# One part of a two-block network: low parts of two projections and the skip product move from VectorE to GpSimd, the decay rows' DMAs from GpSimd to SyncE

## The chip, the cores and the metric

One core of one Trainium2 chip. The metric is the device time of one launch in microseconds, the median over the runs. The engines: TensorE (PE) multiplies matrices, VectorE (DVE), ScalarE (ACT) and GpSimd (POOL) work on tiles, SyncE (SP) only issues DMAs here, GpSimd issues a few as well.

## The reference

Two network blocks for 256 tokens of width 1024, all in float32. The first has retention and attention and a PEER layer (product-key experts); the second has a SwiGLU, a mixer, another SwiGLU and a gated per-layer embedding. The change lies in the mixer of the second block:

```python
proj = n @ w_in[i]
u, v, z, xbc, dt_raw = jnp.split(proj, IN_SPLITS_2, axis=-1)
ya = chunked_spatial_gating(jax.nn.gelu(u, approximate=False), jax.nn.gelu(v, approximate=False), ...)
ya = rmsnorm(ya, gm_out_norm[i])
yb = mamba2_mixer(z, xbc, dt_raw, conv_w[i], conv_b[i], dt_bias[i], a_log[i], d_skip[i], ssm_norm[i])
h = h + jnp.concatenate([ya, yb], axis=-1) @ w_out[i]
...
xbc = jax.nn.silu(causal_depthwise_conv(xbc, conv_w, conv_b))
dt = jax.nn.softplus(dt_raw.astype(f32) + dt_bias.astype(f32))
y = ssd_chunked(xs, dt, a, bm, cm) + xs * d_skip.astype(f32)[:, None]
```

`ssd_chunked` takes exponentials of differences of the cumulated decays (16 heads, two chunks of 128 tokens), masks them and multiplies with C B^T, and that with x dt. The last line's second term is the skip product.

## The kernel before

The kernel streams all weights once from DRAM, in 257 chunks of 1 MB (`wall`, 128 x 2048 floats), through a ring of three buffers (`raw`). Each chunk is two halves, called units and numbered 0 to 513 through the whole program. A float32 matmul is done in three passes at float32r: the weights are split into a high part `w_hi` (ScalarE's copy of `raw`, rounded) and a low part `w_lo = raw - w_hi`, and the activations likewise (tiles `HX`, `HC`). Both parts have a ring of `NH` = 4 halves. The road of one unit: SyncE loads the chunk (`sync_program`; it waits until the low parts of the chunk three back are made), ScalarE makes the high part (`ahead` in `scalar_program`; it waits until TensorE has used the unit four back), and VectorE, or GpSimd if the unit is in the set `LO_POOL`, makes the low part (`ahead` in `vector_program` and `gpsimd_program`). TensorE begins a unit with the matmuls of the high part (semaphore `s_hi`) and waits for the low part (`LOW[u]`, counted by `s_lov` for VectorE, `s_lop` for GpSimd) before the last third. `ahead(u)` makes parts up to three units beyond u (`REACH`, `AHEAD` = 3), one after the other in the engine's own order.

Before the change `LO_POOL` holds 27 units, all between the first block's query projection and the first PEER units, where VectorE seeks the top 16.

The mixer has three stretches. The xBC projection (`U_XBC`, units 386 to 397) gives six bank loads of two blocks of 128 features, c = 0 to 5; for each VectorE evacuates the bank with the norm's factor (`tt(xbT..)`, signal `s_xb`), ScalarE makes the first of four taps of the convolution, VectorE the other three (`convolved(m)`, twelve m, three `stt` of 128x256 each), and ScalarE the Silu (`activated(m)`). TensorE needs the evacuation of pair c before pair c + 2. At c = 1 the softplus of dt is made, in small steps that go back and forth between VectorE and ScalarE. The second projection (`U_IN2`, units 398 to 421) has six groups of four units: v, v, u, u (Gelu) and z, z (Silu). Beside them the rest of the mixer is done, in steps named in the table `SIDE`: one row for each unit from 398 on, which all engines go through in the same order, each doing its own share. The names that matter: `silu` and `conv` are the last convolved blocks; `xt` and `xs` turn x to token rows; `cb` and `cbs` are C B^T; `xdt` is x dt; `dec` makes the differences of decays for four heads from `R`, rows of the cumulated decays broadcast to all partitions; `exp` and `mt` make the masked matrix from them, `heads` multiplies it with xdt; `xd` is the skip product (in place in `xs`), `y` adds it to the heads; `vneg` to `vc` are the layer norm of v, `gm` and `gmu` the spatial gate, `ub..` and `yb..` the blocks of the output projection (`U_OUT2`, units 422 to 437).

`R` comes by DRAM: GpSimd waits for ScalarE's copy of the turned decays (`s_act`), writes 16 KB to `acs_keep` and reads two broadcasts of 1 MB back:

```python
p.wait_ge(s_act, 1)
e.dma_start(acs_keep.rearrange("(h t) -> h t", h=16), acT[0:16, :, :].rearrange("p a b -> p (a b)")).then_inc(s_keep, 16)
p.wait_ge(s_keep, 48)
for b in range(2):
    e.dma_start(R[b], acs_keep[b * 2048:(b + 1) * 2048].partition_broadcast(128)).then_inc(s_R, 16)
```

The instructions are written by helpers, so that the profile has one line for many: L923 is every matmul, L1524 every ScalarE operation, L1992 every `tensor_tensor` of VectorE, L1997 and L1999 `tensor_scalar`, L2004 `scalar_tensor_tensor`, L2769 GpSimd's low part. Nearly all working tiles lie in one arena and are called `ar` in the profile. Each engine waits for its own last result before the next instruction (`settle`), but where a call says `free`.

Of the kernel before, what the change touches and what calls it, by code (L numbers as in the profile page):

```python
# [122 lines left out]
def ffn_at(base, c):  # L123
# [8 lines left out]
           | set(range(U_PEER + 20, U_PEER + 25)))  # L132
# [196 lines left out]
def group_done(g):  # L329
# [17 lines left out]
    [("act", 0), ("silu", 8), ("conv", 10)],  # L347
# [12 lines left out]
    [("heads", 4), ("xd", 0)],  # L360
    [("xd", 1), ("y", 0)],
# [43 lines left out]
def program(nc, wall, keys_d, cols_d, rows_d, bigrows_d, crow_d, wmod_d, dist_d, x_d, ctx_d, pT_d, gws_d, out_d, n_chunks):  # L405
    assert n_chunks * 2 == U_END
    with ExitStack() as es:
# [36 lines left out]
        class Arena:  # L444
# [3 lines left out]
            def get(self, *shape, dt=None):  # L448
# [10 lines left out]
                if len(shape) == 3:  # L459
# [1054 lines left out]
        def scalar_program(e):  # L1514
# [387 lines left out]
            def beside(name, n):  # L1902
# [13 lines left out]
                elif name == "vsq":  # L1916
                    a.wait_ge(s_vc, 1)
                    for i in range(2):
                        act(m_y[:, i, :], m_v[:, i, :], ACT.Square, bias=lnst[:, i:i + 1], acc=lnst[:, 2 + i:3 + i],
                            sig=s_vsq)  # L1920
                elif name == "vroot":
                    a.wait_ge(s_vv, 1)
                    act(lnst[:, 2:4], lnst[:, 2:4], ACT.Sqrt, sig=s_vs)
                elif name == "usq":
                    a.wait_ge(s_um, 4)
                    for i in range(2):
                        act(big[:, i * 1024:(i + 1) * 1024], m_u[:, i, :], ACT.Square, acc=lnst[:, 4 + i:5 + i],
                            sig=s_usq)
                elif name == "uroot":
                    a.wait_ge(s_uv, 1)  # L1930
                    act(lnst[:, 4:6], lnst[:, 4:6], ACT.Sqrt, sig=s_us)
                elif name == "ubh":
                    high(TB_U + n)
                elif name == "ysq":
                    for g_ in range(2):
                        a.wait_ge(s_yz, 2 * g_ + 2)
                        for i in range(2):
                            act(big[:, i * 1024 + g_ * 512:i * 1024 + (g_ + 1) * 512], m_y[:, i, g_ * 512:(g_ + 1) * 512],
                                ACT.Square, acc=lnst[:, 6 + 2 * i + g_:7 + 2 * i + g_], sig=s_ysq)
                elif name == "yroot":  # L1940
                    a.wait_ge(s_yv, 1)
                    act(lnst[:, 6:10], lnst[:, 6:10], ACT.Sqrt, sig=s_ys)
                elif name == "ybh":
                    high(TB_Y + n)
# [40 lines left out]
        def vector_program(e):  # L1985
# [622 lines left out]
            def beside(name, n):  # L2608
# [9 lines left out]
                elif name in ("xdt", "xd"):  # L2618
                    xv = xs[:, n, :].rearrange("p (h d) -> p h d", d=64)
                    if name == "xdt":  # L2620
                        v.wait_ge(s_xs, 4)
                        tt(xdt[:, n, :].rearrange("p (h d) -> p h d", d=64), xv, bc(dt[:, n, :], 2, 64), MUL, sig=s_xdt)
                    else:
                        tt(xv, xv, bc(row("dskip"), 2, 64), MUL)
# [20 lines left out]
                elif name == "y":  # L2645
                    s_ = slice(n * 512, (n + 1) * 512)
                    v.wait_ge(s_yh, 2 * n + 2)
                    for i in range(2):
# [6 lines left out]
                elif name == "vvar":  # L2655
                    v.wait_ge(s_vsq, 2)
                    ts(lnst[:, 2:4], lnst[:, 2:4], 1.0 / 1024, EPS, MUL, ADD, sig=s_vv)
                elif name == "vrcp":
                    v.wait_ge(s_vs, 1)
# [13 lines left out]
                elif name == "uvar":  # L2673
                    v.wait_ge(s_usq, 2)
                    ts(lnst[:, 4:6], lnst[:, 4:6], 1.0 / 1024, EPS, MUL, ADD, sig=s_uv)
                elif name == "uscale":
                    v.wait_ge(s_us, 1)
# [10 lines left out]
                elif name == "yvar":  # L2688
                    v.wait_ge(s_ysq, 4)
                    ts(lnst[:, 6:10], lnst[:, 6:10], 1.0 / 512, EPS, MUL, ADD, sig=s_yv)  # L2690
                elif name == "yscale":
                    v.wait_ge(s_ys, 1)
# [62 lines left out]
        def gpsimd_program(e):  # L2755
# [37 lines left out]
            p.did(e.memset(xbT[:, :, 0:4], 0.0), s_set)  # L2793
            p.wait_ge(s_big, 32)
# [127 lines left out]
```

## Time and profile before

| | us |
|---|---|
| median of 3 runs | 1695.77 |
| lowest, highest | 1695.45, 1696.73 |
| profiled execution, its span from first to last instruction | 1695.0 |
| TensorE matmuls busy | 1631.9 (96%) |
| VectorE busy | 1270.3 (75%) |
| ScalarE busy | 967.3 (57%) |
| GpSimd busy | 72.6 (4%) |

The profiled execution has no separate end-to-end time; its span lies 0.8 us under the median of the runs. Busy shares overlap: an engine can be busy all the time and set nothing. What sets the time is read from the waits of TensorE, stage by stage.

### The profile page before, as it was taken

Reading aid. Unit: us, or ns where it says so; the run is one execution under the profiler, and the core shown is the slowest. Engines: PE = TensorE matmul, PEld = TensorE weight load, DVE = VectorE, ACT = ScalarE, POOL = GpSimd, SP = SyncE. Lnnn points to the kernel's source line nnn. Section 1 sums busy time; section 2 is a strip of 40 time slices with the busy share of each in tenths; the row PEclk is TensorE's granted clock in tenths of the full one; section 3 lists DMA queues with packets and bytes.
Section 4 is the critical chain, followed back from the end, with each engine's and each line's share of the span. In section 5 each row is a group of like instructions: output and inputs, shape, how many; then the busy total and the mean of one; then the engine's idle time right before and its main releaser. Section 6 shows DMA issues by size and latency. Waiting matters only on the chain.

```text
span 1695.0 us, 26902 instructions
## 1 busy us (share of the span) xinstructions
PE 1631.9 (96%) x10312; PEld 1392.9 (82%) x10312; DVE 1270.3 (75%) x2044; ACT 967.3 (57%) x1342; POOL 72.6 (4%) x46
## 2 busy tenths in 40 slices
PE   7999889998999999999999999999998989999997
PEld 2777679998999888888888888788888778788886
DVE  3668766999888999987777666776667887676666
ACT  5546655554555454555555555655556867655556
POOL 0000007520000000000000000000000000000000
PEclk9999889999999999999999999999999999999999
DMA  8644235446555455566655555455543533555552
GB/s 336 253 173 160 90 120 192 162 166 208 192 185 191 174 192 213 193 255 219 219 208 210 214 198 197 152 199 192 197 179 139 223 124 128 202 199 179 198 195 75
DMA packets 53266, 317.86 MB, mean 188 GB/s; under 512 B 5937, under 2 KB 6097, under 8 KB 19218
## 3 DMA queue, kind: packets, MB, share of 16 engines
q1 hardware_dynamic: 51954, 310.08, 51.3%
q0 software_dynamic: 1184, 6.05, 0.9%
q8 instruction: 82, 1.34, 0.3%
q14 instruction: 46, 0.38, 0.1%
HBM read 306.65 MB, written 9.47 MB: 186 GB/s over the span
## 4 chain that ended last, share of the span: by engine, by line
PE 79%; DVE 14%; ACT 4%; DMA 2%; issue 1%; SPq 0%; DVEq 0%; ACTq 0%; POOL 0%
PE pb L923 78%; DVE w_lo L1992 4%; DVE ar L1992 4%; ACT ar L1524 2%; DVE ar L2004 2%; DVE ar L2373 1%; ACT w_hi L1524 1%; DVE ar L2370 1%; DMA raw<-in_wall 1%; DMA ar<-acs_keep 1%; DVE ar L2377 1%; ACT L1524 0%; DVE ar L2148 0%; DVE ar L2008 0%; DVE sm L2226 0%
## 5 line engine op out<-in xcount | busy, mean ns | idle before, releaser
L1992 DVE TENSOR_TENSOR w_lo<-raw,w_hi 128x1024 fp32r<-128x1024 f32 x471 | 577.0, 1225 | 174.5 <-ACT w_hi L1524 143.2
L1524 ACT ACTIVATE w_hi<-raw 128x1024 fp32r<-128x1024 f32 x498 | 528.7, 1062 | 153.2 <-PE pb L923 112.8
L923 PE MATMUL pb<-HX,w_hi 128*128 128x256 f32 (+1 forms) x2752 | 509.1, 332 | 7.6 <-DVE HX L1992 3.4
L923 PEld LDWEIGHTS pb<-HX,w_hi 128*128 128x128 f32 x2752 | 413.8, 192 | 50.9 <-issue 3.9
L923 PE MATMUL pb<-w_hi,HC 128*128 128x512 f32 (+1 forms) x1648 | 444.5, 391 | 2.9 <-DVE HC L2004 1.8
L923 PEld LDWEIGHTS pb<-w_hi,HC 128*128 128x128 f32 x1648 | 302.7, 189 | 64.0 <-issue 3.9
L1524 ACT ACTIVATE ar<-pb 128x256 f32<-128x256 f32 (+2 forms) x320 | 152.6, 477 | 328.5 <-PE pb L923 226.0
L1992 DVE TENSOR_TENSOR ar<-ar 128x512 bf16<-128x512 bf16 (+9 forms) x506 | 268.6, 566 | 43.8 <-ACT ar L1524 19.9
L923 PE MATMUL pb<-HX,w_lo 128*128 128x256 f32 x1952 | 279.8, 284 | 2.5 <-DVE w_lo L1992 2.2
L923 PEld LDWEIGHTS pb<-HX,w_lo 128*128 128x128 f32 x1952 | 264.4, 192 | 14.5 <-DVE w_lo L1992 3.3
L923 PE MATMUL pb<-w_lo,HC 128*128 128x512 f32 (+1 forms) x824 | 253.2, 389 | 0.0
L923 PEld LDWEIGHTS pb<-w_lo,HC 128*128 128x128 f32 x824 | 154.8, 189 | 32.5
L923 PE MATMUL pb<-w_hi,HX 128*128 128x512 f32 x512 | 141.5, 398 | 2.8 <-ACT w_hi L1524 2.0
L923 PE MATMUL pb<-ar 128*128 128x64 bf16 (+3 forms) x1960 | 122.6, 222 | 10.9 <-issue 3.6
L923 PEld LDWEIGHTS pb<-ar 128*128 128x128 bf16 (+2 forms) x1960 | 103.4, 119 | 32.5 <-issue 21.7
L923 PEld LDWEIGHTS pb<-w_hi,HX 128*128 128x128 f32 x512 | 93.2, 188 | 23.1 <-ACT w_hi L1524 3.1
L1524 ACT ACTIVATE HC<-ar 128x512 fp32r<-128x512 f32 (+1 forms) x89 | 55.4, 623 | 83.3 <-PE pb L923 46.9
L1992 DVE TENSOR_TENSOR ar<-pb,ar 128x512 f32<-128x512 f32 (+1 forms) x86 | 58.4, 679 | 52.6 <-ACT ar L1524 44.6
L1524 ACT ACTIVATE ar<-ar 128x512 f32<-128x512 f32 (+7 forms) x108 | 66.1, 612 | 55.6 <-DVE ar L1992 31.5
L1992 DVE TENSOR_TENSOR HC<-ar,HC 128x512 fp32r<-128x512 f32 (+1 forms) x89 | 60.5, 680 | 32.8 <-ACT HC L1524 28.1
L923 PE MATMUL pb<-w_lo,HX 128*128 128x512 f32 x256 | 79.7, 392 | 0.6 <-DVE w_lo L1992 0.3
L2769 POOL TENSOR_TENSOR w_lo<-raw,w_hi 128x1024 fp32r<-128x1024 f32 x27 | 64.8, 2401 | 104.1 <-ACT w_hi L1524 91.5
(148 smaller groups left out, 674.3 us busy)
## 6 DMA issues: line engine op xcount, KB each, us to landing
raw<-in_wall SPq DMA_DIRECT2D x257, 1024.0 KB, 4.8
ar<-in_wmod SPq DMA_DIRECT2D x24, 512.0 KB, 4.3
act_keep<-ar SPq DMA_DIRECT2D x28, 256.0 KB, 5.6
ar<-act_keep SPq DMA_DIRECT2D x28, 256.0 KB, 5.0
x<-in_wmod SPq DMA_DIRECT2D x8, 512.0 KB, 5.6
ar<-in_bigrows POOLq DMA_DIRECT2D x2, 1024.0 KB, 5.1
ar<-acs_keep POOLq DMA_DIRECT2D x2, 1024.0 KB, 9.0
x<-in_x SPq DMA_DIRECT2D x1, 1024.0 KB, 12.1
```

Of the source, the lines that this page charges most:

```text
L923: return e.matmul(o, l, r, start=start, stop=stop, skip_group_check=True)
L1524: a.did(e.activation(out, in_, func, scale=scale, **kw), sig)
L1992: v.did(e.tensor_tensor(out, a_, b_, op), sig)
L2004: v.did(e.scalar_tensor_tensor(out, a_, s_, b_, op0, op1), sig)
L2370: v.did(e.max(vals[:, c_], src))
L2373: v.did(e.max_index(idx[:, c_], vals[:, c_], src))
L2377: v.did(e.match_replace(src, vals[:, c_], src, NEG))
L2769: p.did(e.tensor_tensor(w_lo[:, made % NH, :], raw_half(w), w_hi[:, made % NH, :].bitcast(F32), SUB), s_lop)
```

## The change

Units 388 to 421 join `LO_POOL`: all but the first two low parts of the xBC projection and all of the second projection's are GpSimd's. The skip product `xd` leaves `SIDE` and VectorE and becomes `skipped(i)` on GpSimd, ahead of the low parts of units 409 and 412; `y` waits for both (`s_xd`). GpSimd's affine select (the causal mask of the gate's weights) now stands behind four low parts. The DMAs of the decay rows are issued by SyncE, after the chunks of units 406 and 408. In `SIDE` the step `conv 11` moves up by one unit and `silu 11` from the fourth row to the third, so that it stands before the first Gelu. Semaphores of the variances are merged (one counter for several steps, with the counts to match), which is left out below.

```diff
 LO_POOL = (set(range(U_QUERY + 4, U_PEER + 5)) | set(range(U_PEER + 7, U_PEER + 12))
-           | set(range(U_PEER + 20, U_PEER + 25)))
+           | set(range(U_PEER + 20, U_PEER + 25)) | set(range(U_XBC + 2, U_IN2 + 24)))
...
 SIDE = [
-    [("act", 0), ("silu", 8), ("conv", 10)],
-    [("xt", 0), ("xt", 1), ("silu", 9), ("conv", 11)],
-    [("xt", 2), ("xt", 3), ("xs", 0), ("silu", 10)],
-    [("xt", 4), ("xt", 5), ("xs", 1), ("silu", 11)],
+    [("act", 0), ("silu", 8), ("conv", 10), ("conv", 11)],
+    [("xt", 0), ("xt", 1), ("silu", 9)],
+    [("xt", 2), ("xt", 3), ("xs", 0), ("silu", 10), ("silu", 11)],
+    [("xt", 4), ("xt", 5), ("xs", 1)],
     [("xt", 6), ("xt", 7), ("xs", 2), ("dec", 0)],
...
-    [("heads", 4), ("xd", 0)],
-    [("xd", 1), ("y", 0)],
+    [("heads", 4)],
+    [("y", 0)],
...
                 e.dma_start(raw[:, n % NRAW, :], wall[n]).then_inc(s_raw[n % NRAW], 16)
+                if n == U_IN2 // 2 + 4:
+                    e.wait_ge(s_act, 1)
+                    e.dma_start(acs_keep.rearrange("(h t) -> h t", h=16),
+                                acT[0:16, :, :].rearrange("p a b -> p (a b)")).then_inc(s_ckeep, 16)
+                if n == U_IN2 // 2 + 5:
+                    e.wait_ge(s_ckeep, 32)
+                    for b in range(2):
+                        e.dma_start(R[b], acs_keep[b * 2048:(b + 1) * 2048].partition_broadcast(128)).then_inc(s_R, 16)
...
                     v.wait_ge(s_yh, 2 * n + 2)
+                    v.wait_ge(s_xd, 2)
                     for i in range(2):
                         tt(m_y[:, i, s_], PB[4 + i][:, :], xs[:, i, s_], ADD, sig=s_y)
...
             p.did(e.memset(xbT[:, :, 0:4], 0.0), s_set)
+            ahead(U_XBC + 2)
             p.wait_ge(s_big, 32)
             p.settle()
             p.did(e.affine_select(out=gw, in_=gw, pattern=[[0, 8], [1, 128]], compare_op=ALU.is_ge, fill=0.0, base=0,
                                   channel_multiplier=-1), s_set)
-            p.wait_ge(s_act, 1)
-            e.dma_start(acs_keep.rearrange("(h t) -> h t", h=16), acT[0:16, :, :].rearrange("p a b -> p (a b)")).then_inc(s_keep, 16)
-            p.wait_ge(s_keep, 48)
-            for b in range(2):
-                e.dma_start(R[b], acs_keep[b * 2048:(b + 1) * 2048].partition_broadcast(128)).then_inc(s_R, 16)
+
+            def skipped(i):
+
+                xv = xs[:, i, :].rearrange("p (h d) -> p h d", d=64)
+                p.settle()
+                p.did(e.tensor_tensor(xv, xv, bc(row("dskip"), 2, 64), MUL), s_xd)
+
+            ahead(U_IN2 + 7)
+            p.wait_ge(s_xdt, 2)
+            skipped(0)
+            ahead(U_IN2 + 10)
+            skipped(1)
+            ahead(U_IN2 + 20)
             p.wait_ge(s_res, result(N_F2, 1, 1))
```

VectorE before, from the last full set of six convolution steps (`ar<-ar,cols`) through the two half sets of `conv 10` and `conv 11` to the decays of `dec 0` (128x4 to 128x1024) and the first of `cbs`:

```order
L2004 SCALAR_TENSOR_TENSOR ar<-ar,cols 128x256 x6
L1992 TENSOR_TENSOR w_lo<-raw,w_hi 128x1024
L2004 SCALAR_TENSOR_TENSOR ar<-ar,cols 128x256 x3
L1992 TENSOR_TENSOR w_lo<-raw,w_hi 128x1024
L2004 SCALAR_TENSOR_TENSOR ar<-ar,cols 128x256 x3
L1992 TENSOR_TENSOR w_lo<-raw,w_hi 128x1024 x3
L1992 TENSOR_TENSOR ar<-ar 128x4
L1992 TENSOR_TENSOR ar<-ar 128x4x2x128
L1992 TENSOR_TENSOR ar<-ar 128x512
L1997 TENSOR_SCALAR ar<-ar 128x1024
L1992 TENSOR_TENSOR w_lo<-raw,w_hi 128x1024 x2
L1992 TENSOR_TENSOR ar<-pb,cols 128x2x128 x2
```

The same place in the change:

```order
L2011 SCALAR_TENSOR_TENSOR ar<-ar,cols 128x256 x12
L1999 TENSOR_TENSOR ar<-ar 128x4
L1999 TENSOR_TENSOR ar<-ar 128x4x2x128
L1999 TENSOR_TENSOR ar<-ar 128x512
L2004 TENSOR_SCALAR ar<-ar 128x1024
L1999 TENSOR_TENSOR ar<-pb,cols 128x2x128 x2
```

Every `w_lo` row is gone, and convolution steps and decays stand next to each other. GpSimd in the change, from the DMAs of the mixer's constants on (before, the rows with `w_lo` and with `ar<-ar,rows` were not there, and three DMAs with `acs_keep` stood behind the affine select):

```order
L2796 DMA ar<-in_bigrows 128x2048
L2797 DMA ar<-in_gws 128x1024
L2798 MEMSET ar 128x12x4
L2774 TENSOR_TENSOR w_lo<-raw,w_hi 128x1024 x4
L2802 AFFINE_SELECT ar<-ar 128x1024
L2774 TENSOR_TENSOR w_lo<-raw,w_hi 128x1024 x17
L2809 TENSOR_TENSOR ar<-ar,rows 128x1024
L2774 TENSOR_TENSOR w_lo<-raw,w_hi 128x1024 x3
L2809 TENSOR_TENSOR ar<-ar,rows 128x1024
L2774 TENSOR_TENSOR w_lo<-raw,w_hi 128x1024 x10
L2818 DMA ar<-in_bigrows 128x2048
```

The two skip products stand between low parts, so that whatever they wait for holds up the low parts behind them.

## Rows read from the trace of the kernel before

**Rows 1.** The page: span and busy time of each engine.

```profile
span 1695.0 us, 26902 instructions
...
PE 1631.9 (96%) x10312; PEld 1392.9 (82%) x10312; DVE 1270.3 (75%) x2044; ACT 967.3 (57%) x1342; POOL 72.6 (4%) x46
```

**Rows 2.** Busy time by stretch: stretch, length, engines, granted clock (1.00 is full), DMA.

```profile
1306.70:1310.30 3.60, 3.59 (x19) 3.59 (x20) 2.91 (x6) 3.33 (x6) 0.00 (x0) 0.61 0.00 0
...
1343.00:1358.20 15.20, 15.16 (x68) 12.39 (x68) 13.13 (x14) 12.12 (x14) 0.00 (x0) 1.00 0.50 192
...
1386.00:1390.00 4.00, 4.00 (x19) 3.92 (x20) 3.86 (x5) 0.00 (x0) 0.00 (x0) 0.57 0.33 135
```

**Rows 3.** Timeline of TensorE: start, duration, what [idle before it, releaser].

```profile
1306.71 3.17 PE L923 MATMUL pb<-HX,w_hi 128*128 128x256 f32 x16 [2.37 <-DVE ar L1992]
...
1343.04 1.57 PE L923 MATMUL pb<-ar 128*128 128x256 f32 x8 [1.83 <-ACT ar L1524]
...
1347.19 1.07 PE L923 MATMUL pb<-w_hi,HX 128*128 128x512 f32 x4
...
1349.91 1.07 PE L923 MATMUL pb<-w_hi,HX 128*128 128x512 f32 x4
...
1386.00 3.65 PE L923 MATMUL pb<-ar 128*128 128x128 f32 x16 [3.35 <-DVE ar L1992]
...
1414.49 0.62 PE L923 MATMUL pb<-w_lo,HX 128*128 128x512 f32 x2
```

**Rows 4.** Timeline of VectorE in the convolutions.

```profile
1305.97 0.69 DVE L1992 TENSOR_TENSOR ar<-pb,fsc 128x512 f32<-128x512 f32 x1
...
1313.92 0.69 DVE L1992 TENSOR_TENSOR ar<-pb,fsc 128x512 f32<-128x512 f32 x1
1314.72 3.15 DVE L2004 SCALAR_TENSOR_TENSOR ar<-ar,cols 128x256 f32<-128x256 f32 x6
1317.98 2.55 DVE L1992 TENSOR_TENSOR w_lo<-raw,w_hi 128x1024 fp32r<-128x1024 f32 x2
```

**Rows 5.** Groups of VectorE by shape, 1283 to 1409: busy us, mean ns | idle before.

```profile
L1992 DVE TENSOR_TENSOR w_lo<-raw,w_hi 128x1024 fp32r<-128x1024 f32 x33 | 40.4, 1225 | 17.9 <-ACT w_hi L1524 15.3
L2004 DVE SCALAR_TENSOR_TENSOR ar<-ar,cols 128x256 f32<-128x256 f32 x36 | 17.4, 484 | 2.5 <-DVE w_lo L1992 0.5
L1992 DVE TENSOR_TENSOR ar<-ar 128x1024 f32<-128x1024 f32 x6 | 7.3, 1225 | 0.3
L1992 DVE TENSOR_TENSOR ar<-ar 128x1536 f32<-128x1536 f32 x3 | 5.3, 1758 | 0.3
L2004 DVE SCALAR_TENSOR_TENSOR ar<-ar 128x1024 f32<-128x1024 f32 x4 | 5.1, 1285 | 0.2
...
L1997 DVE TENSOR_SCALAR ar<-ar 128x1024 f32<-128x1024 f32 x4 | 2.8, 694 | 0.1
L1992 DVE TENSOR_TENSOR ar<-ar 128x512 f32<-128x512 f32 x4 | 2.8, 691 | 0.1
```

**Rows 6.** Timeline, VectorE and GpSimd in the first block's top-16 stretch.

```profile
319.96 2.71 DVE L2370 MAX8 ar<-ar 128x8 f32<-128x256 f32 x8
320.01 12.60 POOL L2769 TENSOR_TENSOR w_lo<-raw,w_hi 128x1024 fp32r<-128x1024 f32 x5 [10.14 <-DVE w_lo L1992]
```

**Rows 7.** Timeline around GpSimd's affine select.

```profile
1280.68 1.11 POOL L2796 TENSOR_SCALAR_AFFINE_SELECT ar<-ar 128x1024 f32<-128x1024 f32 x1 [5.30 <-DMA ar<-in_gws]
...
1281.14 0.73 DVE L1997 TENSOR_SCALAR fsc<-cols,sm 128x128 f32<-128x128 f32 x1
...
1282.18 0.29 DVE L1997 TENSOR_SCALAR fsc<-cols,sm 128x128 f32<-128x128 f32 x1
```

**Rows 8.** Timeline of ScalarE between the first Gelu and the last Silu.

```profile
1341.28 1.28 ACT L1524 ACT_TABLE_LOAD   x1
```

**Rows 9.** The decay rows: GpSimd's issue (timeline), and a link of the chain of waits.

```profile
1332.11 0.50 POOL L2799 DMA_DIRECT2D acs_keep<-ar  x1 [50.31 <-ACT ar L1524]
...
1334.60 10.83 DMA ar<-acs_keep
```

More of the change, by code:

```diff
@@ L1919, in beside @@
                         act(m_y[:, i, :], m_v[:, i, :], ACT.Square, bias=lnst[:, i:i + 1], acc=lnst[:, 2 + i:3 + i],
-                            sig=s_vsq)
+                            sig=s_sq)
                 elif name == "vroot":
-                    a.wait_ge(s_vv, 1)
-                    act(lnst[:, 2:4], lnst[:, 2:4], ACT.Sqrt, sig=s_vs)
+                    a.wait_ge(s_var, 1)
+                    act(lnst[:, 2:4], lnst[:, 2:4], ACT.Sqrt, sig=s_root)
                 elif name == "usq":
@@ L1927, in beside @@
                         act(big[:, i * 1024:(i + 1) * 1024], m_u[:, i, :], ACT.Square, acc=lnst[:, 4 + i:5 + i],
-                            sig=s_usq)
+                            sig=s_sq)
                 elif name == "uroot":
-                    a.wait_ge(s_uv, 1)
-                    act(lnst[:, 4:6], lnst[:, 4:6], ACT.Sqrt, sig=s_us)
+                    a.wait_ge(s_var, 2)
+                    act(lnst[:, 4:6], lnst[:, 4:6], ACT.Sqrt, sig=s_root)
                 elif name == "ubh":
@@ L1938, in beside @@
                             act(big[:, i * 1024 + g_ * 512:i * 1024 + (g_ + 1) * 512], m_y[:, i, g_ * 512:(g_ + 1) * 512],
-                                ACT.Square, acc=lnst[:, 6 + 2 * i + g_:7 + 2 * i + g_], sig=s_ysq)
+                                ACT.Square, acc=lnst[:, 6 + 2 * i + g_:7 + 2 * i + g_], sig=s_sq)
                 elif name == "yroot":
-                    a.wait_ge(s_yv, 1)
-                    act(lnst[:, 6:10], lnst[:, 6:10], ACT.Sqrt, sig=s_ys)
+                    a.wait_ge(s_var, 3)
+                    act(lnst[:, 6:10], lnst[:, 6:10], ACT.Sqrt, sig=s_root)
                 elif name == "ybh":
@@ L2617, in beside @@
                     cp(cbs[:, :, 256:384], PB[4][:, :].rearrange("p (a b) -> p a b", a=2)[:, :, 128:256], sig=s_cbs)
[L2618 to L2624, printed above, removed]
+                elif name == "xdt":
+                    v.wait_ge(s_xs, 4)
+                    tt(xdt[:, n, :].rearrange("p (h d) -> p h d", d=64), xs[:, n, :].rearrange("p (h d) -> p h d", d=64),
+                       bc(dt[:, n, :], 2, 64), MUL, sig=s_xdt)
                 elif name == "dec":
@@ L2655, in beside @@
                 elif name == "vvar":
-                    v.wait_ge(s_vsq, 2)
-                    ts(lnst[:, 2:4], lnst[:, 2:4], 1.0 / 1024, EPS, MUL, ADD, sig=s_vv)
+                    v.wait_ge(s_sq, 2)
+                    ts(lnst[:, 2:4], lnst[:, 2:4], 1.0 / 1024, EPS, MUL, ADD, sig=s_var)
                 elif name == "vrcp":
-                    v.wait_ge(s_vs, 1)
+                    v.wait_ge(s_root, 1)
                     rcp(lnst[:, 2:4], lnst[:, 2:4])
@@ L2673, in beside @@
                 elif name == "uvar":
-                    v.wait_ge(s_usq, 2)
-                    ts(lnst[:, 4:6], lnst[:, 4:6], 1.0 / 1024, EPS, MUL, ADD, sig=s_uv)
+                    v.wait_ge(s_sq, 4)
+                    ts(lnst[:, 4:6], lnst[:, 4:6], 1.0 / 1024, EPS, MUL, ADD, sig=s_var)
                 elif name == "uscale":
-                    v.wait_ge(s_us, 1)
+                    v.wait_ge(s_root, 2)
                     rcp(lnst[:, 4:6], lnst[:, 4:6])
@@ L2688, in beside @@
                 elif name == "yvar":
-                    v.wait_ge(s_ysq, 4)
-                    ts(lnst[:, 6:10], lnst[:, 6:10], 1.0 / 512, EPS, MUL, ADD, sig=s_yv)
+                    v.wait_ge(s_sq, 8)
+                    ts(lnst[:, 6:10], lnst[:, 6:10], 1.0 / 512, EPS, MUL, ADD, sig=s_var)
                 elif name == "yscale":
-                    v.wait_ge(s_ys, 1)
+                    v.wait_ge(s_root, 3)
                     rcp(lnst[:, 6:10], lnst[:, 6:10])
```

8 lines of the change are left out of this document (3 added, 5 removed).

## The prediction

> **What bounds the kernel now.** I read the page first: the span is 1695.0 us, and TensorE is busy for 96% of it, VectorE for 75%, GpSimd for 4% [rows 1]. So on the whole TensorE sets the time, and a change elsewhere is worth only what TensorE waits for. The next view is the table by stage, and in it the mixer, from the first unit of the xBC projection (1276 us) to the last unit of the second projection (1416 us). I number the halves of weight chunks as the program does: xBC is units 386 to 397, the second projection 398 to 421. The change hands 388 to 421 to GpSimd. TensorE has three holes here worth naming, and the timeline of TensorE tells who ended them. It stands for 2.37 us before 1306.71, and VectorE's evacuation of a bank (ar from pb) ends it; for 1.83 us before 1343.04, ended by ScalarE (the Silu of the last convolved block); for 3.35 us before 1386.00, ended by VectorE (the y sums) [rows 3]. Behind the first and the third the granted clock is 0.61 over 3.6 us and 0.57 over 4 us, where it is 1.00 in the undisturbed stretch from 1343 to 1358 [rows 2]: the clock has fallen to its lower level for a part of those stretches. That costs about 0.39 x 3.6 = 1.4 and 0.43 x 4 = 1.7 us more. With some 1.5 us of holes under 0.7 us, about 12 us can be had in this stage and no more. A unit of the second projection takes 2.72 us where nothing is late (1347.19 to 1349.91) [rows 3].
>
> VectorE is what is late. In the convolutions its rhythm for two units is 0.69 (bank) + 3.15 (six convolution steps) + 2.55 (two low parts) and the gaps, from 1313.92 over 1314.72 and 1317.98 to 1320.53, some 6.7 us with the gap to the next bank [rows 4].
>
> **The change, part by part.**
>
> Low parts off VectorE: 34 of 1.225 us, 33 of them (40.4 us) between 1283 and 1409 [rows 5], and two skip products, by the row of the same shape 1.22 each. VectorE is given back 44 us.
>
> Low parts on GpSimd: the two-input subtraction of 128x1024 takes 2.40 there, and five in a row take 12.60, so (12.60 - 2.40) / 4 = 2.55 us from start to start [rows 6]. 34 of them are 86.7 us, two skip products of the same shape 5.1. GpSimd must make one in each 2.72 us of TensorE; alone on its road it can, just. ScalarE's high parts come up to four units ahead, so the 1.2 us more per low part are covered by that lead (8 us).
>
> The road. GpSimd and VectorE both read and write SBUF, and one place of this trace shows them together on instructions of the kind that matter: GpSimd's affine select (1.11 us from 1280.68) ends at 1281.79, and VectorE's TENSOR_SCALAR of 128x128 that began at 1281.14 takes 0.73 us, ending at 1281.87. The same instruction one microsecond later takes 0.29 [rows 7]. It stood still until GpSimd was done. Against that, GpSimd's 27 low parts of before keep their 2.40 us, but beside them VectorE ran only MAX8 and its kin, with one input [rows 6]. No row shows a VectorE instruction with two SBUF inputs beside a low part on GpSimd, and such ones are nearly all that VectorE keeps here. Bounds for them: free of each other (the 27 low parts' 2.40), or one after the other (the TENSOR_SCALAR). I take one after the other. The row is nearer: both instructions want SBUF operands at full rate, while the MAX8 rows want one stream.
>
> The Trainium skill (SBUF — State Buffer, Who interferes with whom) says the same in general: a VectorE instruction with two SBUF inputs, or in a mode that uses both its ports, and a GpSimd instruction that reads SBUF exclude one another for a whole instruction. By that rule the sum is the slower one below; if the rule were wrong for two inputs, it would be the first rival's. This trace agrees for the 0.73 us row; for two inputs no run here shows it yet.
>
> The sum for the excluded road. From 1283 on GpSimd needs it for 33 x 2.55 + 5.1 = 89.3 us. VectorE needs it for 17.4 (36 convolution steps) + 7.3 + 5.3 + 5.1 + 2.8 + 2.8 (decays, products, layer norm) [rows 5], and about 4.7 for some 25 small instructions of 0.16 to 0.3 us: 45.4. Together 134.7 us, with what reads PSUM left out. If the road never rests, the low part of unit 421 is there at 1417.7; TensorE asked for it at 1414.49 [rows 3]. That is +3 us and the floor. It will rest: a low part can't start before its high part, which waits for TensorE's use of the buffer four units back, and VectorE waits for ScalarE (exponentials, Silus). With the road taken for nine tenths the time is 149.7 us and the end 1432.7, +18 us. A second way: in the convolutions the rhythm becomes 0.69 + 3.15 + 2 x 2.55 = 8.9 in place of 6.7, and counting from 1306 along the instructions I am some 6 us late by unit 400. From there to the first product of the heads VectorE has seven instructions of 0.18 to 1.76 us on the decays' chain, each of which may find a low part under way (about four do, 2.4 each): 10 us more, 16 in all. I take **+17 us**. Upper end: all 35 GpSimd instructions hold VectorE for their full 2.41 us (84 us on its remaining 63, and 10 of waits): 157 us, +25, and a few microseconds for TensorE's clock, which fell after holes of 2.4 and 3.4 us: +30.
>
> Decay rows. Before, GpSimd sends acs_keep at 1332.11 and the broadcasts land 10.83 us behind 1334.60 [rows 9]. SyncE now sends them after the chunks of units 406 and 408, so not before the low parts of 401 and 403 are made, with the loads of 1 MB ahead of them in its own queue. If the stage ran as fast as in the first rival, I put the issue at 1331 and the landing where it was, 1342 to 1345: worth nothing, covered by units 404 to 408. In the slow case the low part of 403 is at about 1344 and the rows land 9 us late; TensorE is late by 6 anyway, and the rest is within the 10 us above. GpSimd's two DMA issues (0.5 us) go away with no one waiting.
>
> Silu of the last blocks ahead of the Gelu: one table load of 1.28 us less on ScalarE [rows 8], and the hole at 1343.04 loses its cause (1.8 us), if the convolutions come in time; in the slow case they don't. The skip products on GpSimd wait for VectorE's xdt, with the low parts of units 409 and later queued behind them; the y sums now wait for GpSimd. Both have several microseconds to spare if nothing else is late. The merged semaphores change no wait: nothing.
>
> **The rivals.**
>
> (a) *The two engines don't hinder each other.* Then all three holes close. Counting along: the bank of the third pair is free at 1304.0 in place of 1306.66 (1305.97 + 0.69) [rows 4], since VectorE no longer stands before and in two low parts inside its softplus; unit 398 starts 3 us earlier, and the rest runs at TensorE's rate, with GpSimd busy for 76% of its time: the 12 us less a microsecond or two of new holes, -11 us, 1684.8. For it: 27 low parts with not one stretched. Against it: [rows 7]. Chance 0.21.
>
> (b) *Only the one-input instructions that run fast are excluded, as in rows 7.* VectorE has four of 128x1024 (0.69 us) and a dozen small ones; each may lose up to 2.4, about 5 us on the path: -6, 1689.8. Chance 0.06.
>
> (c) *Excluded, but covered.* VectorE's instructions fall mostly into GpSimd's pauses, and the closed holes pay for the rest: within 3 us of before. Against it: the floor of +3 with no pause at all. Chance 0.06.
>
> (d) *GpSimd is slow with no quarrel over the road.* It decides where a low part with its high part (2.55 + 1.06) comes later than the lead of three units (8.2 us) allows, once ScalarE's side work of 5 us stands ahead; some six places with 1 to 2 us each, less what VectorE gives back: up to +4, 1700. Chance 0.02 for more than +3.4.
>
> **How the numbers follow.** 0.2% of 1695.8 is 3.4 us, about what a measurement of this kernel can tell from nothing. The profiled span is 1695.0 and the median 1695.77; the 0.8 us around it I carry over. The forecast is 1695.8 + 17 = **1712.8 us**, chance 0.65, its own range 1700 to 1726 (+5 to +30). With (d), slower has 0.67; (a) and (b) make faster 0.27; (c) makes the same 0.06. Since a quarter of the chance lies on the faster side, the range reaches there: 1685 to 1726.
>
> **What would show it.** In the profile of the changed kernel the convolution steps (128x256, 484 ns now) and the decays would have longer records beside low parts: a mean well over 484 ns, single ones near 2.9 us, with GpSimd's stretched too where VectorE came first. TensorE's holes between 1300 and 1420 would be more and longer, ended by GpSimd's w_lo or by VectorE's ar. The evacuations' rhythm would be 8 to 9 us and the last unit would end near 1433. I am wrong if the convolution steps still take 484 ns and low parts 2.40 us beside them: then TensorE runs at 2.72 us a unit, its three holes are gone, and the time is near 1685.

## The result, and the profile after

The changed kernel takes 1708.14 us (median of 4 runs, 1706.95 to 1708.9) beside 1696.25 us for the kernel before (4 runs, 1695.45 to 1698.35): ratio 1.0068, 95% interval 1.0056 to 1.008, so 12 us slower. The forecast was 17 us slower.

The head of the page of after, to be read against [rows 1]:

```profile
span 1705.1 us, 26903 instructions
...
PE 1636.6 (96%) x10312; PEld 1397.5 (82%) x10312; DVE 1273.3 (75%) x2008; ACT 965.4 (57%) x1341; POOL 166.4 (10%) x79
```

This one line holds most of the story. VectorE has 36 instructions fewer (2044 to 2008), each of some 1.22 us, 44 us of work, and is as busy as before: 1270.3 us then, 1273.3 now. GpSimd is busy for 94 us more. The 44 us that VectorE was given back, and 3 more, it spent again on something.

The groups of VectorE by shape, 1283 to 1424, show on what (busy us, mean ns of one | idle before); they answer to [rows 5]:

```profile
L2011 DVE SCALAR_TENSOR_TENSOR ar<-ar,cols 128x256 f32<-128x256 f32 x36 | 35.2, 977 | 2.1
L2011 DVE SCALAR_TENSOR_TENSOR ar<-ar 128x1024 f32<-128x1024 f32 x4 | 11.2, 2808 | 0.2
L1999 DVE TENSOR_TENSOR ar<-ar 128x1024 f32<-128x1024 f32 x6 | 9.5, 1590 | 0.3
L1999 DVE TENSOR_TENSOR ar<-ar 128x512 f32<-128x512 f32 x4 | 8.9, 2234 | 0.1
...
L2004 DVE TENSOR_SCALAR ar<-ar 128x1024 f32<-128x1024 f32 x4 | 6.9, 1733 | 0.1
L2011 DVE SCALAR_TENSOR_TENSOR ar<-pb,cols,ar 128x128 f32<-128x128 f32 x16 | 4.5, 345 | 0.4
L1999 DVE TENSOR_TENSOR ar<-ar 128x4 f32<-128x4 f32 x4 | 4.4, 1092 | 7.9 <-DMA ar<-acs_keep 7.7
...
L1999 DVE TENSOR_TENSOR ar<-pb,fsc 128x512 f32<-128x512 f32 x5 | 3.5, 692 | 7.8 <-PE pb L930 7.3
```

The convolution step (two SBUF inputs) took 484 ns and now 977 in the mean; the layer norm's 128x1024 took 1285 and now 2808; the one-input TENSOR_SCALAR of 128x1024 694 and now 1733. The two forms with an input from PSUM (`pb`) keep their 345 and 692 ns (343 and 692 before). GpSimd's own groups, 1270 to 1424:

```profile
L2774 POOL TENSOR_TENSOR w_lo<-raw,w_hi 128x1024 fp32r<-128x1024 f32 x34 | 90.6, 2665 | 46.8 <-ACT w_hi L1531 43.8
L2809 POOL TENSOR_TENSOR ar<-ar,rows 128x1024 f32<-128x1024 f32 x2 | 4.7, 2336 | 1.2 <-DVE ar L1999 1.2
```

The two timelines side by side, VectorE's and then GpSimd's (start, duration, what, idle before it):

```profile
1296.78 2.54 DVE L1999 TENSOR_TENSOR ar<-ar 128x32 f32<-128x32 f32 x2
...
1305.51 3.16 DVE L2011 SCALAR_TENSOR_TENSOR ar<-ar,cols 128x256 f32<-128x256 f32 x6
1308.77 0.69 DVE L1999 TENSOR_TENSOR ar<-pb,fsc 128x512 f32<-128x512 f32 x1
1309.57 11.32 DVE L2011 SCALAR_TENSOR_TENSOR ar<-ar,cols 128x256 f32<-128x256 f32 x6
1320.99 0.69 DVE L1999 TENSOR_TENSOR ar<-pb,fsc 128x512 f32<-128x512 f32 x1
1321.78 3.16 DVE L2011 SCALAR_TENSOR_TENSOR ar<-ar,cols 128x256 f32<-128x256 f32 x6
...
1325.84 15.96 DVE L2011 SCALAR_TENSOR_TENSOR ar<-ar,cols 128x256 f32<-128x256 f32 x12
...
1349.54 5.22 DVE L1999 TENSOR_TENSOR ar<-ar 128x4 f32<-128x4 f32 x3 [7.73 <-DMA ar<-acs_keep]
...
1379.68 11.34 DVE L2011 SCALAR_TENSOR_TENSOR ar<-ar 128x1024 f32<-128x1024 f32 x4
```

```profile
1310.06 10.02 POOL L2774 TENSOR_TENSOR w_lo<-raw,w_hi 128x1024 fp32r<-128x1024 f32 x4 [10.79 <-ACT w_hi L1531]
1325.05 7.39 POOL L2774 TENSOR_TENSOR w_lo<-raw,w_hi 128x1024 fp32r<-128x1024 f32 x3 [4.97 <-ACT w_hi L1531]
...
1383.43 19.01 POOL L2774 TENSOR_TENSOR w_lo<-raw,w_hi 128x1024 fp32r<-128x1024 f32 x6
```

Six steps at 1305.51 and six at 1321.78, while GpSimd rests, take 3.16 us as before. Six at 1309.57, beside four low parts, take 11.32: 8.2 us more, 2.0 us for each low part. Taken singly, four of the six last 2.44 to 2.65 us, and each of these ends 0.28 us behind the low part that it met, while the four low parts keep their 2.4 us. How long VectorE's instruction is makes no difference to what it loses: in the softplus one of the two instructions of 128x32 at 1296.78 takes 2.31 us in place of 0.19, as much loss as with the larger steps. GpSimd stands 10.79 us without work ahead of the four low parts and then has them one after the other, since ScalarE makes the high parts in the order of its own program and stood there 8.66 us, to 1305.44, for the bank that VectorE evacuates at 1304.71. Then ScalarE makes the high parts two and two, and GpSimd's low parts come in bunches. So the two engines do not mesh, they collide in convoys.

TensorE's holes, to be read against [rows 3]:

```profile
1305.46 3.67 PE L930 MATMUL pb<-HX,w_hi 128*128 128x256 f32 x16 [2.90 <-DVE ar L1999]
...
1325.03 1.33 PE L930 MATMUL pb<-w_hi,HX 128*128 128x512 f32 x4 [2.55 <-ACT w_hi L1531]
1327.47 1.22 PE L930 MATMUL pb<-w_lo,HX 128*128 128x512 f32 x2 [1.11 <-POOL w_lo L2774]
1347.24 1.55 PE L930 MATMUL pb<-ar 128*128 128x256 f32 x8 [2.44 <-ACT ar L1531]
...
1362.75 0.73 PE L930 MATMUL pb<-w_lo,HX 128*128 128x512 f32 x2 [1.26 <-POOL w_lo L2774]
1367.43 5.38 PE L930 MATMUL pb<-ar 128*128 128x64 f32 x24 [2.56 <-DVE ar L1999]
...
1428.72 2.05 PE L930 MATMUL pb<-w_hi,HX 128*128 128x512 f32 x4 [2.91 <-issue]
```

Before, three holes were above 1.2 us, now six. The first product of the heads (24 matmuls) takes 5.38 us where it took 2.89, because the clock fell behind the hole ahead of it. The table by stage (stretch, length, PE, PEld, DVE, ACT, POOL, granted clock, DMA share, GB/s), to be read beside [rows 2]:

```profile
1305.40:1309.00 3.60, 3.54 (x17) 3.54 (x18) 3.14 (x8) 3.29 (x6) 0.00 (x0) 0.53 0.00 0
1340.00:1352.00 12.00, 9.56 (x47) 7.74 (x46) 4.02 (x7) 9.74 (x15) 5.96 (x3) 1.00 0.68 265
1367.40:1373.00 5.60, 5.57 (x25) 5.57 (x26) 5.17 (x7) 3.02 (x5) 2.18 (x1) 0.50 0.39 133
```

At 0.53 and 0.50 the engine ran at its lower level, 1.2 GHz, for nearly all of those stretches, the first behind a hole of 2.90 us, the second behind one of 2.56 us.

For a ledger I count from TensorE's first xBC matmul, as the program ahead of it is the same in all kernels but started it between 1273.6 and 1276.3 us in the profiled executions. Before (first matmul at 1276.13): first heads' product 82.2 us behind it, end of the span 418.9. After (1274.34): 93.1 and 430.8. So TensorE is 10.9 us late at the heads and 11.9 at the end, which is the measured 12.

SyncE's queue carries the decay rows now. Its timeline, then the landing from the chain of waits; they answer to [rows 9]:

```profile
1332.90 0.42 SPq L898 DMA_DIRECT2D acs_keep<-ar  x1
1339.44 0.34 SPq L895 DMA_DIRECT2D raw<-in_wall  x1
1339.84 0.90 SPq L903 DMA_DIRECT2D ar<-acs_keep  x2
```

```profile
1340.31 9.20 DMA ar<-acs_keep
```

They land at 1349.5, 75.2 us behind the first matmul instead of 69.3, and VectorE stands 7.73 us for them.

### The profile page after: what moved, and what is told of

It reads as the page before. It is cut to its first block, busy times and chain, and to the rows that moved or that the text cites. A ratio compares the mean times of both kernels' runs of the same rounds, so it can differ in the third digit from the quotient of the medians.

```text
span 1705.1 us, 26903 instructions
## 1 busy us (share of the span) xinstructions
PE 1636.6 (96%) x10312; PEld 1397.5 (82%) x10312; DVE 1273.3 (75%) x2008; ACT 965.4 (57%) x1341; POOL 166.4 (10%) x79
## 4 chain that ended last, share of the span: by engine, by line
PE 78%; DVE 15%; ACT 4%; DMA 1%; issue 1%; POOL 0%; SPq 0%; DVEq 0%; ACTq 0%; POOLq 0%
PE pb L930 78%; DVE ar L1999 4%; DVE ar L2011 3%; DVE w_lo L1999 2%; ACT ar L1531 2%; DVE ar L2380 1%; ACT w_hi L1531 1%; DVE ar L2377 1%; DMA raw<-in_wall 1%; ACT L1531 1%; DVE ar L2004 1%; DMA ar<-acs_keep 1%; DVE ar L2384 1%; DVE ar L2155 0%; DVE ar L2015 0%
## 5 line engine op out<-in xcount | busy, mean ns | idle before, releaser
L1999 DVE TENSOR_TENSOR w_lo<-raw,w_hi 128x1024 fp32r<-128x1024 f32 x437 | 535.5, 1225 | 158.4 <-ACT w_hi L1531 129.6
L1999 DVE TENSOR_TENSOR ar<-ar 128x512 bf16<-128x512 bf16 (+9 forms) x506 | 286.7, 601 | 54.4 <-ACT ar L1531 23.2
L2774 POOL TENSOR_TENSOR w_lo<-raw,w_hi 128x1024 fp32r<-128x1024 f32 x61 | 155.4, 2548 | 150.2 <-ACT w_hi L1531 106.4
L930 PE MATMUL pb<-w_hi,HX 128*128 128x512 f32 x512 | 145.5, 407 | 7.0 <-ACT w_hi L1531 3.9
```

Source lines behind the costliest of these rows:

```text
L930: return e.matmul(o, l, r, start=start, stop=stop, skip_group_check=True)
L1999: v.did(e.tensor_tensor(out, a_, b_, op), sig)
L2774: p.did(e.tensor_tensor(w_lo[:, made % NH, :], raw_half(w), w_hi[:, made % NH, :].bitcast(F32), SUB), s_lop)
```

## The experiments

Twelve kernels, each timed beside the kernel before on the same chip. In the first group that kernel had a median of 1696.66 us, in the second 1696.9, in the third 1696.04.

### Low parts back on VectorE

```diff
-           | set(range(U_PEER + 20, U_PEER + 25)) | set(range(U_XBC + 2, U_IN2 + 24)))
+           | set(range(U_PEER + 20, U_PEER + 25)))
```

> The changed kernel with the 34 low parts back on VectorE; skip products on GpSimd, decay rows from SyncE and the Silus ahead of the Gelu stay. Theory (the low parts on GpSimd shut VectorE's two-input instructions out, and nothing else costs): the 12 us go, and the Silu's table load and the skip products give 1 to 4 us, so 1692 to 1695. Rival (the decay rows, which land 6 us later than before, are part of the loss): some 3 to 5 us remain, 1699 to 1701. The convolution steps go back to 0.48 us either way.

Measured: 1700.8 us, ratio 1.0026 (1.0015 to 1.0037). The convolution step is back at 485 ns. But without a single low part on GpSimd the kernel is still 4 us slower than before, and VectorE shows where:

```profile
1346.17 2.15 DVE L1999 TENSOR_TENSOR ar<-ar 128x4 f32<-128x4 f32 x3 [4.31 <-DMA ar<-acs_keep]
```

So the decay rows are likely to cost by themselves, which my sum had at nothing; the kernel without low parts and with early rows, below, shows it.

### The decay rows sent by GpSimd again

SyncE's part of the rows goes; in GpSimd's program, with the low parts left on it:

```diff
+            ahead(U_IN2)
+            p.wait_ge(s_act, 1)
+            e.dma_start(acs_keep..., acT[0:16, :, :]...).then_inc(s_keep, 16)
+            p.wait_ge(s_keep, 48)
+            for b in range(2):
+                e.dma_start(R[b], acs_keep[...].partition_broadcast(128)).then_inc(s_R, 16)
             ahead(U_IN2 + 7)
```

> The changed kernel with the decay rows sent by GpSimd again, right behind the low part of unit 401. Theory (the exclusion alone): VectorE waits 7.7 us for the rows in the changed kernel, but TensorE is late anyhow; within 1 us of the changed kernel's 1708. Rival (late rows are part of the loss): the rows land some 5 us earlier, VectorE's wait of 7.7 us shrinks to 2 or 3, and the time falls by 3 to 5 us, to 1703 to 1705.

Measured: 1702.6 us, ratio 1.0037 (1.0023 to 1.0051), 5.5 us less than after. The convolution step takes 939 ns still. In the chain of waits the rows land at 1344.7, 69.8 us behind the first matmul:

```profile
1332.97 3.97 DMA acs_keep<-ar
1337.78 6.94 DMA ar<-acs_keep
```

With this the 12 us part into some 5.5 for the rows and 6.5 for the rest.

### One input in place of two

```diff
-                    stt(cvT[:, m, :], xbT[:, m, 1 + k:257 + k], cw[:, m, k:k + 1], cvT[:, m, :], ...)
+                    one(cvT[:, m, :], xbT[:, m, 1 + k:257 + k], ...)
```

`one` is a TENSOR_REDUCE over a last axis of length one, that is, a copy: both kernels leave out the multiplications and additions, so their output is another. Likewise for the other two-input instructions named below. In after:

> The changed kernel, in which VectorE's convolution steps, decay differences, mt, xdt and the layer norm of v are replaced by one-input reductions over an axis of one, of the same element counts (a copy: the multiplications and additions are left out, so the output is another). Theory (two SBUF inputs are what excludes): each lasts as it does with GpSimd idle, low parts 2.4 us, TensorE's holes in the mixer mostly gone, and this kernel is 7 to 12 us faster than its counterpart on the kernel before, near 1685. Rival (GpSimd's longer low parts or the order of its work are the cause): it stays 10 us or more slower than the counterpart, near 1708.

And the same edit in before:

> The kernel before with the same one-input replacements, as the counterpart. Both theories: the same durations within 5%, so within 2 us of the kernel before, 1694 to 1698.

Measured: 1685.73 us (ratio 0.9934, 0.9921 to 0.9948) and 1697.55 us (1.0005, 0.9996 to 1.0014). The pair with two inputs differs by +12, the pair with one by -11.8. Group rows of the changed kernel, VectorE and GpSimd:

```profile
L2019 DVE TENSOR_REDUCE ar<-ar 128x256 f32<-128x256 f32 x36 | 15.1, 420 | 2.1
...
L2004 DVE TENSOR_SCALAR ar<-ar 128x1024 f32<-128x1024 f32 x4 | 4.5, 1131 | 0.1
...
L2775 POOL TENSOR_TENSOR w_lo<-raw,w_hi 128x1024 fp32r<-128x1024 f32 x34 | 81.8, 2407 | 38.1 <-ACT w_hi L1531 34.4
```

The reduce takes 420 ns in both kernels, beside low parts and without them; GpSimd's low part falls from 2665 to 2407 ns. The TENSOR_SCALAR, one input but a fast form, which this edit left alone, is still stretched, 694 to 1131. The small two-input instructions, left alone as well, are held up in the same kernel: one of 128x32 takes 2.30 us in place of 0.19, while 22 reductions of 128x256 that overlap GpSimd's work stay at 421 ns. So the second SBUF input is the quarrel, and the fast one-input form is in it as well. The -11.8 is what rival (a) gave the change if there were none: -11.

### GpSimd writes only

```diff
-                        p.did(e.tensor_tensor(w_lo[...], raw_half(w), w_hi[...].bitcast(F32), SUB), s_lop)
+                        p.did(e.memset(w_lo[...].bitcast(F32), 0.0), s_lop)
```

> The kernel after with GpSimd's 34 low parts replaced by memsets of the same 128x1024 tiles: GpSimd writes as much, reads nothing, so the output lacks the low parts' share. Theory (it is GpSimd's reading of SBUF that shuts VectorE's two-input instructions out): convolution steps 484 ns beside them, VectorE busy some 40 us less than now, late rows still there: 1690 to 1697. Rival (any GpSimd instruction on SBUF shuts them out): steps stretched by about a memset's own length each time, 1700 or more.

The low parts are zero here, the subtraction is left out. Measured: 1680.41 us, ratio 0.9908 (0.9893 to 0.9923), faster than I had for either theory, as I had let the late rows cost. A group of VectorE, then from the timeline a TENSOR_SCALAR, an evacuation and the wait for the rows, and the page:

```profile
L2011 DVE SCALAR_TENSOR_TENSOR ar<-ar,cols 128x256 f32<-128x256 f32 x36 | 17.5, 485 | 2.1
...
1298.85 0.46 DVE L2006 TENSOR_SCALAR ar<-ar 128x32 f32<-128x32 f32 x1
...
1303.66 0.69 DVE L1999 TENSOR_TENSOR ar<-pb,fsc 128x512 f32<-128x512 f32 x1
...
1336.99 2.15 DVE L1999 TENSOR_TENSOR ar<-ar 128x4 f32<-128x4 f32 x3 [11.87 <-DMA ar<-acs_keep]
...
PE 1624.5 (97%) x10312; PEld 1390.9 (83%) x10312; DVE 1229.1 (73%) x2008; ACT 965.4 (57%) x1341; POOL 107.7 (6%) x79
```

Convolution steps of 485 ns beside 0.95 us memsets (18 of the 36 overlap one): a GpSimd instruction that reads nothing stretches none of them. The skip product on GpSimd, which reads, still holds up a product of 128x1536 in the same kernel, 3.50 us in place of 1.76. VectorE's busy time falls by 41 us against before. The Trainium skill (SBUF — State Buffer, Who interferes with whom) says the same: two-input VectorE instructions contend with GpSimd instructions that read SBUF, not with ones that only write. The memsets are also shorter than low parts, so part of the 16 us is that; the pair above, with GpSimd at 2407 ns, has the clean figure. The fast one-input form is another matter: the TENSOR_SCALAR of 128x32 at 1298.85 took 0.46 us beside a memset, in place of 0.18, and ended with it, and the memset that began during a TENSOR_SCALAR of 128x1024 took 1.23 us in place of 0.95. No other TENSOR_SCALAR there overlaps a memset.

The rows wait is a lesson of its own. VectorE stands 11.87 us for them here, and the kernel is the fastest of all: TensorE needed nothing from it yet. A long wait is a loss only when someone waits behind it.

### The rows one place earlier in SyncE's queue

```diff
                                 acT[0:16, :, :].rearrange("p a b -> p (a b)")).then_inc(s_ckeep, 16)
-                if n == U_IN2 // 2 + 5:
                     e.wait_ge(s_ckeep, 32)
```

> The kernel after with the broadcast of the decay rows in SyncE's program one chunk earlier: right behind acs_keep, not behind the next weight chunk. Theory (what costs 5 us is the place in SyncE's queue: 1332.90 for acs_keep, 1339.84 for the rows, behind a chunk that waits for a low part): the rows are issued near 1335 and land near 1344.5, VectorE's wait of 7.73 us shrinks to about 3, time 1702 to 1704, as with GpSimd sending them. Rival (SyncE's queue delivers them late behind its megabytes whatever their place): landing near 1349, 1707 to 1709.

Measured: 1703.05 us, ratio 1.0042 (1.0028 to 1.0055), 5 us less than after by one line. SyncE's timeline and VectorE's wait:

```profile
1332.48 0.42 SPq L898 DMA_DIRECT2D acs_keep<-ar  x1
1337.02 0.81 SPq L902 DMA_DIRECT2D ar<-acs_keep  x2
1339.03 0.33 SPq L895 DMA_DIRECT2D raw<-in_wall  x1
...
1344.13 3.34 DVE L1998 TENSOR_TENSOR ar<-ar 128x4 f32<-128x4 f32 x3 [2.74 <-DMA ar<-acs_keep]
```

The rows were issued at 1337.0, not 1335: acs_keep itself takes its time behind the chunks in flight. They landed at 1344.1. SyncE serves them as early as GpSimd does; what cost 5 us was the chunk of units 408 and 409 that stood between the two transfers in a queue kept in order, waiting for a buffer that the late low part of 403 still read.

### Silus early and skip products on GpSimd, nothing else

After with the low parts back and the rows sent by GpSimd (both edits above).

> The kernel after with all 34 low parts back on VectorE and the decay rows sent by GpSimd right behind its affine select, as before: of the change only the early last Silus and the two skip products on GpSimd are left. Theory (late rows from SyncE cost 4 to 5 us, the low parts on GpSimd the rest): 1700.8 - 4.5, so 1696, within 2 us of the kernel before; the rows land near 1345, VectorE stands less than 1 us for them. Rival (what was lost without the low parts, +4, came from the Silus' place or from the skip products, which stretch VectorE's instructions beside them): 1699 to 1701.

Measured: 1697.58 us, ratio 1.0001 (0.9992 to 1.001). With the two parts that cost taken out, no loss is left. From 1700.8 the rows alone are worth 3.2 us here. The skip products still cost at one place: the first stands beside a product of 128x1536 on the chain to the heads, which takes 3.50 us in place of 1.76, and TensorE waits 2.07 us there.

### The early Silus alone

Before, with the first four rows of SIDE as in the change.

> The kernel before with only the order of the side work changed (last convolution one unit earlier, last Silu ahead of the first Gelu). Theory of the prediction: the hole of 1.83 us at 1343.04 closes and a table load of 1.28 us goes, so up to 2 us less, 1694.5 to 1696. Rival: the time waits for the decay rows or for VectorE behind it, and the hole only moves: 1696.7, no change.

Measured: 1694.78 us, ratio 0.999 (0.9981 to 0.9999). In the profile TensorE has no idle time ahead of the masks' product at 1340.66, where before it stood 1.83 us [rows 3]; but it now waits 1.13 us for a low part of VectorE's at 1335.52, so the wait in part only moved, and by the ledger the end is 1.0 us earlier. The 2 us are inside the bound of 0.2% that I set, so this is the direction of the theory and no more.

### Low parts given away in one part of the stage only

Early Silus, skip products on GpSimd, rows from GpSimd, and on it the low parts of units 410 to 421 alone, then also 388 to 391, then 392 to 409 alone:

```diff
+           | set(range(U_IN2 + 12, U_IN2 + 24)))
```

```diff
+           | set(range(U_XBC + 2, U_XBC + 6)) | set(range(U_IN2 + 12, U_IN2 + 24)))
```

```diff
+           | set(range(U_XBC + 6, U_IN2 + 12)))
```

> Early Silus, skip products on GpSimd, decay rows sent by GpSimd early, and GpSimd makes only the low parts of units 410 to 421, behind the convolutions and the first decays. Theory (the loss is where VectorE's two-input work is on the critical chain, the convolutions and decays; later the low parts given away pay): the hole of 3.35 us ahead of the y sums shrinks to under 1 and TensorE's clock stays up behind it, so 3 to 4 us less than the kernel before, 1692 to 1694. Rival (exclusion costs wherever two-input work is near, here four layer norm instructions of 1.28 us and four products): as before or up to 4 us more, 1696 to 1700.

> The same, and GpSimd also makes the low parts of units 388 to 391, ahead of the convolutions. Theory: the hole of 2.37 us ahead of the third pair's bank is shorter by what VectorE is given back there, another 1 to 3 us less: 1690 to 1692. Rival: VectorE's small instructions of the softplus there are held up in turn, the hole stays, 1692 to 1696.

> As the kernel with the rows sent by GpSimd and all 34 low parts on GpSimd (1702.6), with only the 18 low parts of units 392 to 409 on GpSimd, those beside convolutions and decays; the 16 of 388 to 391 and 410 to 421 are back on VectorE. Theory (the loss stands beside the convolutions and decays): 1701 to 1704. Rival (the 34 share it evenly): 1697.6 + 18/34 x 5 = 1700.2 or less.

Measured: 1697.9 us (1.0005, 0.9996 to 1.0014), 1697.3 us (1.0003, 0.9994 to 1.0012), 1701.3 us (1.0029, 1.0018 to 1.0041). So most of the loss stands beside convolutions and decays, but the hoped-for gain elsewhere did not come. In the kernel with 410 to 421, TensorE's timeline says why:

```profile
1364.65 0.73 PE L922 MATMUL pb<-w_lo,HX 128*128 128x512 f32 x2 [1.23 <-POOL w_lo L2766]
1369.08 0.73 PE L922 MATMUL pb<-w_lo,HX 128*128 128x512 f32 x2 [1.42 <-POOL w_lo L2766]
...
1417.31 1.52 PE L922 MATMUL pb<-w_hi,HX 128*128 128x512 f32 x4 [2.91 <-issue]
```

The hole ahead of the y sums (3.35 us before) closed, as I expected. In its place TensorE waits 2.65 us for the first two low parts, which GpSimd makes in 2.4 us where VectorE took 1.23, and 2.91 us at 1417.31 where kernels whose last low parts are VectorE's wait 0.57 to 0.96: this matmul waits for VectorE's and ScalarE's HX blocks. VectorE's last ends at 1417.20, 143.2 us behind the first matmul, where before it was 143.5; TensorE's last heads' product began 2.7 us earlier than before and gained nothing by it. The low parts of 388 to 391 did not shorten the hole ahead of the third pair's bank either: 2.38 us without them, 2.39 with them. Those four were not its cause, but two later low parts may be, which VectorE still makes in the middle of the softplus (at 1294.46 and 1297.50 in the kernel with 388 to 391). The kernel with memsets, where VectorE makes neither and its small instructions are hardly held up, has its third evacuation at 1303.66, 27.4 us behind the first matmul in place of 29.8, and no such hole. With real low parts on GpSimd the small instructions were held up instead, and the hole stood at 2.90 us.

### The skip products later

```diff
             p.wait_ge(s_xdt, 2)
+            p.wait_ge(s_mt, 2)
             skipped(0)
```

> The earlier kernel with early Silus, skip products on GpSimd and the decay rows sent early by GpSimd (1697.6), with one wait more: GpSimd's first skip product waits for the second pair of masked decays, so it no longer stands beside the 128x1536 instructions (1.76 us, stretched to 2.19 in the mean) on the chain to the first product of the heads. Theory: the hole of 2.07 us before that product closes, the y sums stay early: 1693 to 1695.5, below the 1694.8 of the early Silus alone or equal to it. Rival (the skip products only move the hole from the y sums to another place): 1696 to 1698.

Measured: 1697.33 us, ratio 1.0006 (0.9997 to 1.0015). The hole ahead of the heads closed and all four of 128x1536 are back at 1.76 us. The skip products now stand beside the layer norm: its 128x1024 group rose from 1285 to 1650 ns in the mean (one took 2.74 us), and a hole of 2.03 us before 1375.99, for a low part on VectorE, took the place of the other. The rival held. No kernel here beats the one before by more than the 2 us of the early Silus, except those that leave work out.

## Why the prediction came out right, point by point

**The mechanism** was the forecast's: steps well over 484 ns (977), single ones near 2.9 us (the longest 2.65), GpSimd's stretched as well (2665 ns against 2407 undisturbed), TensorE's holes more and longer. The pair with one input shows that it decides the sign: +12 with it, -11.8 without. The one 0.73 us row [rows 7] was the right one to trust, against 27 unhindered low parts [rows 6], whose neighbours had one input. Rival (b), only fast one-input forms, is refuted by the 977 ns; (c) by the 12 us; (d) by the one-input pair, where GpSimd's slowness alone still left 11.8 us of gain.

**The road's term was too large.** I summed 2.55 us of exclusion for every low part and took the road as full for nine tenths. VectorE's 47 us, over 36 moved instructions, are 1.3 us each. Where a low part met a two-input instruction it cost VectorE 2.0 us, beside the convolution steps as beside the layer norm. Two instructions of the layer norm and the two low parts that they met (timeline from 1384.4 to 1387.8):

```profile
1384.40 6.62 DVE L2011 SCALAR_TENSOR_TENSOR ar<-ar 128x1024 f32<-128x1024 f32 x2
1383.43 6.51 POOL L2774 TENSOR_TENSOR w_lo<-raw,w_hi 128x1024 fp32r<-128x1024 f32 x2
```

Each of VectorE's takes 3.29 us in place of 1.285, each low part 3.18 in place of 2.41, and the ends alternate, 1.08 us from GpSimd's to VectorE's and 2.25 from VectorE's to GpSimd's. So they do go one after the other, but a pair takes 3.33 us and not the sum of the records, 3.69: some 0.2 us of each record runs beside the other engine's. Over some 80 instructions of VectorE's and 35 of GpSimd's that is an estimated 20 us of the 134.7, so the floor of +3, which I also held against rival (c), was none. And seven of the 34 low parts met nothing that they hold up, since VectorE read PSUM beside them or stood for a bank, for the decay rows or for ScalarE. The road alone came to 6 to 7 us (the kernel with the rows from GpSimd, 1702.6), not 17.

The second way had a number right by another road. TensorE was 5.0 us late by unit 400 (57.4 us behind the first matmul in place of 52.4) and 6.0 at the masks' product, where I had said 6 by unit 400. But the evacuations did not come every 8 to 9 us: from the third on they came 4.1, 12.2 and 4.1 us apart, and the last was no later than before (50.7 us behind the first matmul, 51.2 before). TensorE was late at unit 399 for a high part, which ScalarE made only after it had stood 5.95 us for the bank evacuated at 1320.99 (a hole of 2.55 us at 1325.03), then for a low part (1.11) and by the lower clock. That the 6 was hit so nearly is luck. Ahead of the heads I put 10 more, and there were 4.9; with the rows sent by GpSimd, TensorE was late by 4.6 at the heads in all (86.7 us behind the first matmul, against 82.2). Nor did the last unit end near 1433: its successor, the last product of the heads, began at 1422.92.

**The decay rows were the term set wrong.** "Worth nothing, the rest is within the 10 us above" was the step. The landing was late by 5.9 us, not 9, and the lateness from the road did not cover it: taken out, it gave 5.5 us back (1708.14 to 1702.6), by moving one line in SyncE's queue 5.1, and 3.2 even with no low part on GpSimd. The sentence for the fast case held: with memsets the rows were issued at 1328.28, landed at 1336.99, and TensorE waited nowhere for them. So did rival (a)'s 1304.0 for the third bank: 1304.35 in that kernel. The two errors have opposite signs, so the total of 17 stands nearer to 12 than its terms deserve; that is luck, and the sign and the mechanism are not.

**The Silus**: the hole at 1343.04 closes when they move alone (1694.78), and in the change it stands, as 2.44 us at 1347.24, since the convolutions come late. As forecast. **The skip products**: not quite nothing. One of the four products of 128x1536, the one on the chain to the first heads, took 3.50 us beside one, in place of 1.76; without low parts and with early rows the sum was still 0.

**Not foreseen** was the last hole. At [rows 3]'s last unit TensorE was 8.4 us late (the last product of the heads behind it at 1422.92, against 1416.31 before). The HX wait at 1428.72 added 2.3, as it grew from 0.64 to 2.91, the same 2.91 as in the four other kernels that keep VectorE's two-input work and have the last low parts on GpSimd. The lower clock behind it added the rest (four matmuls took 2.05 us, 1.17 before).

## What to carry to other kernels

Work moved off a busy engine is a gain only if the engine it goes to does not shut out the first: before giving GpSimd an elementwise job, list what VectorE runs beside it, and count each instruction with two SBUF inputs, or a fast one-input form, as held up for up to 2 us, however short it is, by each GpSimd instruction of this size (2.4 us) that it meets; over all that were moved it came to 1.3 us each. One-input reductions and instructions with one of their inputs in PSUM were free here, and GpSimd's memsets held up no two-input instruction. And a small transfer put into the queue of the big ones inherits every wait of the chunk ahead of it: place it by what stands between it and its reader, not by the number of the chunk.

## What the runs showed of the hardware that I had not expected

- Two-input instructions and low parts alternate strictly, but a pair is shorter than the sum of its records: 3.33 us for 1.285 and 2.41, while GpSimd's low parts beside the short convolution steps kept their 2.4.
- A two-input instruction of 128x32 that takes 0.19 us alone took 2.31 beside a low part: the loss goes with the GpSimd instruction's length, not with VectorE's.
- A memset on GpSimd, which left the convolution steps at 485 ns, did hold up a fast one-input TENSOR_SCALAR of 128x32, 0.46 us in place of 0.18.
- GpSimd's product of 128x1024 with a broadcast row took 1.91 us alone, its low part of the same shape 2.41, its memset 0.95.
- A TENSOR_REDUCE over an axis of length one copied 128x256 in 420 ns, less than the two-input step's 484, and was held up by no low part; it cannot do the step's arithmetic.
